# A hybrid decoder step on one core: operands laid out by the host, wide logits, V sums by head pair, pages among the q tiles

## The chip, the cores and the metric

One core of a Trainium2 chip. The time is the device time of one launch in microseconds, median of three runs: 1452.26 (1451.49 to 1453.10). Rearranging inputs and outputs in numpy on the host is outside it.

## What is computed

One layer on 256 prompt tokens and 32 new tokens (8 sequences of 4), T = 288 together, all in float32: RMSNorm, an input projection to q, k, v (8 heads of 128) and u (1024), block-sparse attention, a pooling mixer on u, an output projection, RMSNorm, a SwiGLU feed-forward of width 5632, a last RMSNorm. Each new token attends to a cache of 2048 keys in 16 pages of 128, from which it takes the best 3 of 8 blocks of 256 keys by the mean key, and to its own block.

```python
k_past = cache_k[page_table].reshape(DB, past, H, D)
k_mean = jnp.mean(kb.astype(jnp.float32), axis=2)
idx, valid = moba_select(qh, q_pos, k_mean)            # top 3 blocks by q . k_mean
s_sel = einsum('bhqd,bhqjkd->bhqjk', q, k_sel) * scale - slope * dist
p = softmax(concatenate([s_sel, s_own]))
o = einsum(p_sel, v_sel) + einsum(p_own, v_own)
...
x = x + concatenate([a, p]) @ w_out
x = x + (silu(h2 @ w_gate) * (h2 @ w_up)) @ w_down
```

The kernel reads every page: all K and V pages of the 8 sequences are 256 pages of 512 KB, 134 MB; the weights are 189 MB.

## The kernel before

Weights come as 360 tiles of 512 KB (`tile_at`), in one order that all engines follow: 16 for q (T_Q), 48 for k, v and u (T_KVU), 16 + 16 for the output projection (T_OP, T_OA), 264 for the feed-forward (T_FF). Each lands in `w_raw` (RAW = 4 slots, 6 in the feed-forward); ScalarE rounds it to `w_hi` (line 610), VectorE takes the rest to `w_lo` (line 877), and TensorE runs 24 matmuls of 288 columns, three to a product (`w_tile`, lines 1504 to 1506). A slot is free for its next load when `w_used` has counted the tile (`slot_free`).

All loads are issued by SyncE, one after the other, each behind its own wait: a wait for a slot holds up everything behind it. The order is that of the `block.sync` part: tables and vectors, x, the q tiles with eight K pages among tiles 6 to 13 (line 493), kvu tiles, then `load_v(0)`, `load_v(1)`, and from line 504 one pass for each unit n: `load_k(n + 2)` when the logits of unit n are done, a V unit when the V sums two units back are done, kvu tiles two units ahead. A unit is four pages of one sequence; K and V are buffered two units deep.

x comes token-major and is turned by TensorE (`x_turned`, 48 transposes) and copied by VectorE (`x_taken`); so are the vectors and the pooling history. q of the new tokens is replicated to four row groups (`replicate_q`, `qrep`, `pad_q`).

For unit (i, j) VectorE turns the four K pages in 32x32 blocks (`turn_k`, line 918). `logits` then runs 4 x 4 x 4 matmuls of 32 rows, 32 columns of q and 256 keys into four banks, one for each row group, which `scaled_logits` adds up. `values(i - 1, j - 1)` runs 8 matmuls (K = 128, 32 columns of probabilities, 512 of V) into banks 6 and 7, four column groups, one to a page; `combine` picks each head's rows with 8 matmuls. A float32 matmul stands as two in the rows. At j = 0 the previous sequence is finished: `block_sums`, `select_blocks` (a chain of twelve small VectorE operations), `joint_max`, exponential, `p_turned`. Between these stand the kvu tiles (units 0 to 23), whose results `take_block` moves out of banks 0 and 1, then the eight heads of the prompt (units 24 to 31), with the mixer's matmuls. The end of the last sequence lies among the T_OP tiles. New K, V and u rows are turned to token-major (`rows_turned` on TensorE for V and u, `turn_keys` on VectorE for K) and stored.

## Time and profile before

| | |
|---|---|
| median of three runs | 1452.26 us |
| profiled execution: span, first to last instruction | 1449.9 us |
| what lies around the span, against the median | 2.4 us |
| TensorE, weight loads, VectorE, ScalarE, GpSimd busy | 1394.4, 1294.3, 901.0, 501.0, 111.7 us |
| moved by the transfers | 334.4 MB, mean 231 GB/s |

Matmuls overlap, so busy time of TensorE is that in which at least one was under way, not a measure of its load. Times in the rows are us from the start of the span. PE is TensorE, PEld its weight loads, DVE VectorE, ACT ScalarE, SPq SyncE's queue; a line number is that of the code.

### The profile page before, as it was taken

What the parts mean: (1) busy time and instruction counts of PE and PEld (TensorE: products, weight loads), DVE (VectorE), ACT (ScalarE), POOL (GpSimd) and SP (SyncE); (2) the same over time, 40 slices, a digit from 0 to 9 for tenths busy, and PEclk for the clock granted to TensorE, in tenths of its full rate; (3) what the DMA queues carried; (4) which work ended last, traced back from release to release, by engine and by line L of the source; (5) the groups of instructions that cost most, each with busy time, mean ns of one, the idle gap of its engine ahead of it and who ended that gap; (6) DMA issues with size and microseconds to landing.
All of it is one profiled execution on the core that took longest, in us unless ns stands there. A gap on an engine that the chain in (4) does not pass through costs nothing.

```text
span 1449.9 us, 34103 instructions
## 1 busy us (share of the span) xinstructions
PE 1394.4 (96%) x13900; PEld 1294.3 (89%) x13900; DVE 901.0 (62%) x1355; ACT 501.0 (35%) x663; POOL 111.7 (8%) x180
## 2 busy tenths in 40 slices
PE   6998998998998999999999999999999999999998
PEld 5986777776756799999999999999999999999997
DVE  4678767767777555787555554546464645555556
ACT  4412122112134234544343433333333333333334
POOL 3226510000000000300000000000000000000002
PEclk9999999999999999999999999999999999999999
DMA  6788999999999855655555555555555555555552
GB/s 215 246 308 305 386 400 400 401 401 392 387 395 375 292 178 179 198 166 190 172 164 165 168 162 171 160 171 161 168 164 166 167 162 170 160 170 162 167 167 95
DMA packets 165096, 334.41 MB, mean 231 GB/s; under 512 B 10335, under 2 KB 54680, under 8 KB 164991
## 3 DMA queue, kind: packets, MB, share of 16 engines
q1 hardware_dynamic: 164999, 333.06, 68.1%
q8 instruction: 68, 1.11, 0.3%
q14 instruction: 29, 0.24, 0.0%
HBM read 328.10 MB, written 5.27 MB: 230 GB/s over the span
## 4 chain that ended last, share of the span: by engine, by line
PE 79%; SPq 10%; DVE 4%; issue 3%; DMA 3%; ACT 1%; DVEq 0%; ACTq 0%
PE banks L1504 24%; PE banks L1505 24%; PE banks L1506 24%; SPq L444 3%; SPq L448 3%; PE banks L1622 2%; SPq L466 2%; PE banks L1604 2%; DVE kpage L918 2%; DMA kpage<-in_cache_k 1%; PE banks L1512 1%; SPq L436 1%; DMA w_raw<-in_w_in 1%; PE banks L1688 0%; SPq L521 0%
## 5 line engine op out<-in xcount | busy, mean ns | idle before, releaser
L877 DVE TENSOR_TENSOR w_lo<-w_raw,w_hi 128x1024 fp32r<-128x1024 f32 x360 | 440.8, 1230 | 423.0 <-ACT w_hi L610 421.7
L1504 PE MATMUL banks<-hh,w_hi 128*128 128x288 f32 x2176 | 647.6, 298 | 3.0 <-DVE w_lo L877 1.8
L1505 PE MATMUL banks<-hl,w_hi 128*128 128x288 f32 x2176 | 645.6, 297 | 0.0
L1506 PE MATMUL banks<-hh,w_lo 128*128 128x288 f32 x2176 | 643.3, 296 | 0.4 <-issue 0.4
L610 ACT ACTIVATE w_hi<-w_raw 128x1024 fp32r<-128x1024 f32 x360 | 379.0, 1059 | 676.1 <-PE banks L1506 448.3
L1504 PEld LDWEIGHTS banks<-hh,w_hi 128*128 128x128 f32 x2176 | 411.7, 189 | 23.0 <-issue 15.2
L1505 PEld LDWEIGHTS banks<-hl,w_hi 128*128 128x128 f32 x2176 | 411.9, 189 | 0.1
L1506 PEld LDWEIGHTS banks<-hh,w_lo 128*128 128x128 f32 x2176 | 410.8, 189 | 0.0
L1506 PE MATMUL banks<-ah,w_lo 128*128 128x288 f32 x704 | 207.8, 295 | 0.0
L1505 PE MATMUL banks<-al,w_hi 128*128 128x288 f32 x704 | 207.4, 295 | 0.0
L1504 PE MATMUL banks<-ah,w_hi 128*128 128x288 f32 x704 | 206.6, 293 | 0.5 <-DVE al L1323 0.5
L918 DVE STREAM_TRANSPOSE kpage<-kpage 128x1024 f32<-128x1024 f32 x128 | 150.8, 1219 | 21.3 <-DMA kpage<-in_cache_k 20.9
L1504 PEld LDWEIGHTS banks<-ah,w_hi 128*128 128x128 f32 x704 | 132.5, 188 | 0.7 <-issue 0.7
L1505 PEld LDWEIGHTS banks<-al,w_hi 128*128 128x128 f32 x704 | 132.4, 188 | 0.0
L1506 PEld LDWEIGHTS banks<-ah,w_lo 128*128 128x128 f32 x704 | 132.2, 188 | 0.0
L1622 PE MATMUL banks<-kpage,qr 32*32 32x256 f32 x4096 | 94.3, 408 | 17.1 <-DVE kpage L918 14.1
L1622 PEld LDWEIGHTS banks<-kpage,qr 32*32 32x32 f32 x4096 | 61.3, 106 | 44.1 <-DVE kpage L918 20.0
L1436 POOL COPY ssq<-sq 128x288 f32<-128x288 f32 x3 | 3.1, 1023 | 925.9 <-ACT sq L627 925.9
L1604 PE MATMUL banks<-vpage,pT 128*32 128x512 f32 x512 | 62.9, 610 | 6.5 <-DMA vpage<-in_cache_v 5.8
L1265 DVE TENSOR_TENSOR xT<-xT,banks 128x288 f32<-128x288 f32 x176 | 67.8, 448 | 0.0
L1439 POOL TENSOR_TENSOR ssq<-ssq,sq 128x288 f32<-128x288 f32 x41 | 44.9, 1095 | 50.3 <-ACT sq L627 46.4
L1604 PEld LDWEIGHTS banks<-vpage,pT 128*32 128x32 f32 x512 | 17.4, 142 | 33.7 <-issue 26.1
(197 smaller groups left out, 637.6 us busy)
## 6 DMA issues: line engine op xcount, KB each, us to landing
kpage<-in_cache_k SPq DMA_DIRECT2D x128, 512.0 KB, 8.0
vpage<-in_cache_v SPq DMA_DIRECT2D x128, 512.0 KB, 7.2
w_raw<-in_w_gate SPq DMA_DIRECT2D x88, 512.0 KB, 3.6
w_raw<-in_w_up SPq DMA_DIRECT2D x88, 512.0 KB, 3.6
w_raw<-in_w_down SPq DMA_DIRECT2D x88, 512.0 KB, 3.7
w_raw<-in_w_in SPq DMA_DIRECT2D x64, 512.0 KB, 9.6
w_raw<-in_w_out SPq DMA_DIRECT2D x32, 512.0 KB, 4.0
xs<-in_x_prompt SPq DMA_DIRECT2D x4, 512.0 KB, 6.1
```

Of the source, the lines that this page charges most:

```text
L444: idx = sp.value_load(pages[0:1, bass.ds(e, 1)], min_val=0, max_val=pool.shape[0] - 1)
L448: sp.dma_start(kpage[:, n % 2, g, :], page(ck, n // NQUADS, 4 * (n % NQUADS) + g)).then_inc(k_in[n % 2][g], 16)
L610: return nc.scalar.activation(out, in_, ACT.Copy)
L877: V.tensor_tensor(w_lo[:, s, :], w_raw[:, s, :], w_hi[:, u, :].bitcast(F32), ALU.subtract).then_inc(lo_ready, 1)
L918: V.transpose(kpage[:, n % 2, g, :], kpage[:, n % 2, g, :]).then_inc(k_turned, 1)
L1265: ins = V.tensor_tensor(xT[:, m0 + m, :], xT[:, m0 + m, :], bank[4 * quad + m][:, 0:T], ALU.add)
L1439: G.tensor_tensor(ssq[:, :], ssq[:, :], sq[:, c % 2, :], ALU.add).then_inc(sq_added, 1)
L1504: PE.matmul(o, wh, xh[:, c, :], start=start and i == 0, stop=False)
L1505: PE.matmul(o, wh, xl[:, c, :], start=False, stop=False)
L1506: last = PE.matmul(o, wl, xh[:, c, :], start=False, stop=stop and i == len(chunks) - 1)
L1604: last = PE.matmul(OB[x][32 * g:32 * g + 32, :], pT[:, g, bass.ds(j, 32, 4)], vpage[:, n % 2, g, 512 * x:512 * x + 512], start=j == 0, sto ...
L1622: last = PE.matmul(S[32 * x:32 * x + 32, a, :], qr[32 * a:32 * a + 32, at_:at_ + 32], keys, start=j == 0 and c == 0, stop=j == NQUADS - 1 ...
```

## The change

The host now lays everything out as it is used. The 360 weight tiles are one array, each tile 4 KB per partition (`weight_tiles`); before, a tile was read in rows of 2 KB, of 1 KB (kvu) or of 512 bytes (T_OP). x comes feature-major in five parts straight into `xT`; the vectors straight into `gains`; the pooling history straight into `ext`; each K page with the head dimension on the partitions, so `turn_k`, `x_turned`, `replicate_q` and the turns of the vectors and the history are gone. `logits` is 8 matmuls a unit (K = 128, 32 columns of q in a strip padded with zeros, 512 keys), four column groups, into bank 2 or 3 by sequence. `values` is 16 matmuls a unit (K = 128, 256 columns: one pair of heads x and x + 4), into one bank; `combine` is 2. The kvu tiles use two pairs of banks in turn. All 16 first pages (K and V units 0 and 1) are issued among the q tiles 4 to 15, behind a wait for the page table. k, v and u are stored as they lie, two large stores between T_OA tiles, and turned by the host.

```diff
-STRIP = 32
+STRIP = 36
 PAD = 3
 
 OA_ORDER = (2, 3, 0, 1)
 NORM2_ORDER = tuple(range(8, 16)) + tuple(range(8))
-X_AHEAD = 3
-
-K_BLOCKS = [(a, b) for b in range(T // 32) for a in range(4)]
...
+PAGES_AT = {k: (1, 1, 2)[k % 3] for k in range(4, 16)}
...
-        qr = sb("qr", [P, 17 * STRIP], stack=kv_a)
-        qrep = sb("qrep", [P, 32, TS], stack=kv_a)
+        qz = sb("qz", [P, 2, H * STRIP], stack=kv_a)
         pages = sb("pages", [1, NB * NPAGES], I32, stack=kv_a)
-        pick = sb("pick", [P, 2], stack=kv_a)
 
...
-        WB = bank[0:2]
-        S = banks[:, 2:6, 0:2 * P]
+        WB = bank[0:2], bank[4:6]
+        SB = bank[2:4]
         HB = bank[0:2]
-        OB = bank[6:8]
-        XB = bank[4], bank[5], bank[7]
+        OB = bank[6][:, 0:2 * DH]
+        block_bank, max_bank, sum_bank = bank[6][:, 256:264], bank[6][:, 264:268], bank[6][:, 268:269]
+        ml_bank = bank[6][0:32, 272:288]
+        PB, comb_bank = bank[7], bank[7][0:32, 0:DH]
 
...
+            sp.dma_start(gains[:, :], A["gains"]).then_inc(gains_in, 16)
+
+            def load_x(n):
+                a, b = X_PARTS[n]
+                sp.dma_start(xT[:, a:b, :], A["x"][:, a:b, :]).then_inc(x_in[n], 16)
+
+            def load(t, free=True):
+
+                n, _, s, _ = t
                 if free:
                     sp.wait_ge(w_used, slot_free(t))
-                k, w = src.shape[0] // P, src.shape[1]
-                sp.dma_start(w_raw[:, s, 0:k * w].rearrange("p (k n) -> p k n", k=k),
-                             src.rearrange("(k p) n -> p k n", p=P)).then_inc(w_in_s[s], 16)
-
+                src = w_d[n] if isinstance(n, int) else w_d[bass.ds(n, 1), :, :].rearrange("a p c -> (a p) c")
+                sp.dma_start(w_raw[:, s, :], src).then_inc(w_in_s[s], 16)
+
+            for k in range(RAW):
+                load_x(k)
+                load(tile_at(T_Q + k), free=False)
+            load_x(RAW)
+            sp.dma_start(tab[:, :], A["tables"]).then_inc(tab_in, 16)
             sp.dma_start(pages[:, :], A["page_table"].rearrange("b n -> (b n)").rearrange("(a n) -> a n", a=1)
                          ).then_inc(pages_in, 16)
+            sp.dma_start(ext[:, :, :, :], A["hist"]).then_inc(hist_in, 16)
+            sp.wait_ge(pages_in, 16)
...
+            first_pages = iter([(load_k_page, 0, g) for g in range(4)] + [(load_k_page, 1, g) for g in range(4)]
+                               + [(load_v_page, 0, g) for g in range(4)] + [(load_v_page, 1, g) for g in range(4)])
+            for k in range(RAW, 16):
+                load(tile_at(T_Q + k))
+                for _ in range(PAGES_AT[k]):
+                    load_page, n, g = next(first_pages)
+                    load_page(n, g)
...
-                    sp.wait_ge(tok_act, 2)
-                    sp.wait_ge(tok_dve, 2)
-                    for part in range(2):
-                        sp.dma_start(vp[part * P:(part + 1) * P, :, :], vtok[:, :, P * part:P * part + P]
-                                     ).then_inc(vtok_stored, 16)
+                    sp.dma_start(wpool[:, :, :, :], A["w_pool"]).then_inc(wpool_in, 16)
...
+                    sp.dma_start(O["pool_sample"], ext[:, :, :, :]).then_inc(pool_stored, 16)
+                    sp.dma_start(O["pool_prompt"], u_last).then_inc(pool_stored, 16)
...
+            sp.wait_ge(z_ready, 24)
+            sp.dma_start(O["k_new"], z[:, ZK:ZK + H, :]).then_inc(kv_stored, 16)
+            sp.dma_start(O["v_new"], z[:, ZV:ZV + H, :]).then_inc(kv_stored, 16)
...
-            def osb_low(b):
-                act.wait_ge(v_done, NQUADS * b + NQUADS)
-                if b:
-
-                    act.wait_ge(comb_done, b)
-                copy(osb[:, 0:512], OB[0][:, :]).then_inc(o6_taken, 1)
...
-            def x_taken(c):
-                dve.wait_ge(xT_in, c + 1)
-                V.tensor_copy(xT[:, c, :], XB[c % 3][:, 0:T]).then_inc(x_ready, 1)
...
-            def turn_k(i, j, pages_=range(4)):
-                n = NQUADS * i + j
-                for g in pages_:
-                    dve.wait_ge(k_in[n % 2][g], 16 * (n // 2) + 16)
-                    V.transpose(kpage[:, n % 2, g, :], kpage[:, n % 2, g, :]).then_inc(k_turned, 1)
...
-            dve.wait_ge(rep_in, 1)
-            for x in range(2):
-                V.tensor_copy(qrep[:, 16 * x:16 * x + 16, :],
-                              OB[x].rearrange("p (s t) -> p s t", t=TS)).then_inc(rep_taken, 1)
-            dve.wait_ge(rep_taken, 2)
...
+            own.link(V.memset(qz[:, :, :], 0.0))
 
             def pad_q(b):
-                V.tensor_copy(qr[:, PAD:PAD + 16 * STRIP].rearrange("p (s q w) -> p s q w", q=NQ, w=4)[:, :, :, 0],
-                              qrep[:, :, NQ * b:NQ * b + NQ]).then_inc(qr_ready, 1)
+                for e in range(2):
+                    V.tensor_copy(qz[:, b % 2, :].rearrange("p (e x s) -> p e x s", e=2, x=4)
+                                  [:, e, :, PAD + 16 * e:PAD + 16 * e + 16].rearrange("p x (q w) -> p x q w", w=4)[:, :, :, 0],
...
                 dve.wait_ge(qk_done, NQUADS * b + NQUADS)
                 if b:
                     dve.wait_ge(pt_in, b)
-                own.did(V.tensor_reduce(d4[:, :, :].rearrange("p a u -> p (a u)"),
-                                        S.rearrange("p a (s k) -> p s a k", s=4), AX.XY, ALU.add))
-                for e in range(2):
-                    for a in range(4):
-                        keys = slice(32 * a, 32 * a + 32)
-                        own.did(V.scalar_tensor_tensor(ss[:, :, keys],
-                                                       S[:, a, P * e:P * e + P].rearrange("p (n i) -> p n i", n=4),
-                                                       pick[:, e:e + 1], (past_bias, ss)[e][:, :, keys],
-                                                       ALU.mult, ALU.add))
-                    own.settle()
-                    if e == 0:
-                        own.link(V.tensor_scalar(d2[:, :], d4[:, 0, :], pair[:, 0:1], None, ALU.mult))
-                own.link(V.scalar_tensor_tensor(d2[:, :], d4[:, 1, :], pair[:, 1:2], d2[:, :], ALU.mult, ALU.add))
+                own.did(V.tensor_reduce(d2[:, :], SB[b % 2].rearrange("p (u k) -> p u k", u=2), AX.X, ALU.add))
+                own.did(V.scalar_tensor_tensor(ss[:, :, :], SB[b % 2].rearrange("p (n r) -> p n r", n=4), SCALE,
+                                               past_bias, ALU.mult, ALU.add))
+                own.settle()
                 V.tensor_tensor(dn[:, :, :], d2[:, :].unsqueeze(1).to_broadcast([P, 4, 2]),
...
+                V.tensor_copy(osb[:, :, :], OB.rearrange("p (e d) -> p e d", e=2)).then_inc(o_taken, 1)
...
-            def x_turned(c):
-                if c >= 3:
-                    pe.wait_ge(x_ready, c - 2)
-                if c == KC // 2:
-                    pe.wait_ge(x_half_in[1], 48)
-                for n in range(3):
-                    rows = P if n < 2 else TS
-                    last = turn(XB[c % 3][:, P * n:P * n + rows], xs[0:rows, n, P * c:P * c + P], rows)
-                last.then_inc(xT_in, 1)
...
-            def replicate_q():
-                pe.wait_ge(rep_table, 1)
-                for c in range(2):
-                    pe.wait_ge(quad_taken[c], QT0)
-                for c in range(4):
-                    last = PE.matmul(OB[c // 2][:, 256 * (c % 2):256 * (c % 2) + 256],
-                                     rep_w[:, c, :, :].rearrange("p a i -> p (a i)"),
-                                     z[:, ZQ:ZQ + H, TP:T].rearrange("p (e x) t -> p x e t", e=2),
-                                     start=True, stop=True)
-                last.then_inc(rep_in, 1)
-
...
-                for x in range(2):
-                    for g in range(4):
-                        last = PE.matmul(OB[x][32 * g:32 * g + 32, :], pT[:, g, bass.ds(j, 32, 4)],
-                                         vpage[:, n % 2, g, 512 * x:512 * x + 512], start=j == 0,
-                                         stop=j == NQUADS - 1)
+                if j == 0 and b:
+                    pe.wait_ge(o_taken, b)
+                for g in range(4):
+                    for x in range(4):
+                        heads = vpage[:, n % 2, g, :].rearrange("p (e x d) -> p e x d", e=2, x=4)
+                        last = PE.matmul(OB[32 * x:32 * x + 32, :], pT[:, g, bass.ds(j, 32, 4)], heads[:, :, x, :],
+                                         start=j == 0 and g == 0, stop=j == NQUADS - 1 and g == 3)
                 last.then_inc(v_done, 1)
...
             def logits(b, j):
                 n = NQUADS * b + j
-                pe.wait_ge(k_turned, 4 * n + 4)
+                pe.wait_ge(k_in[n % 2], 64 * (n // 2) + 64)
                 if j == 0:
-                    pe.wait_ge(qr_ready, b + 1)
-                    if b:
-                        pe.wait_ge(dn_ready, b)
-                for c in range(4):
-                    for a in range(4):
-                        for x in range(4):
-                            at_ = STRIP * (4 * c + x) + PAD - j
-                            keys = kpage[32 * a:32 * a + 32, n % 2, :, :].rearrange(
-                                "p n (e x c i) -> p e x c n i", e=2, x=4, c=4)[:, :, x, c, :, :]
-                            last = PE.matmul(S[32 * x:32 * x + 32, a, :], qr[32 * a:32 * a + 32, at_:at_ + 32], keys,
-                                             start=j == 0 and c == 0, stop=j == NQUADS - 1 and c == 3)
+                    pe.wait_ge(qz_ready, 2 * b + 2)
+                    if b >= 2:
+                        pe.wait_ge(dn_ready, b - 1)
+                keys = kpage[:, n % 2, :, :].rearrange("p n (h r) -> p n h r", h=H)
+                for e in range(2):
+                    for x in range(4):
+                        h = x + 4 * e
+                        at_ = STRIP * h + PAD - j
+                        last = PE.matmul(SB[b % 2][32 * x:32 * x + 32, :], qz[:, b % 2, at_:at_ + 32], keys[:, :, h, :],
+                                         start=j == 0 and e == 0, stop=j == NQUADS - 1 and e == 1)
                 last.then_inc(qk_done, 1)
 
             def kvu_tile(n):
                 m, r = n // 4, n % 4
-                if r == 0 and m:
-
-                    pe.wait_ge(z_ready, 2 * m)
-                w_tile(tile_at(T_KVU + n), CW, range(4 * r, 4 * r + 4), WB, hh, hl, r == 0, r == 3)
+                if r == 0 and m >= 2:
+
+                    pe.wait_ge(z_ready, 2 * m - 2)
+                w_tile(tile_at(T_KVU + n), CW, range(4 * r, 4 * r + 4), WB[m % 2], hh, hl, r == 0, r == 3)
...
-                for h in range(H):
-                    last = PE.matmul(OB[0][0:32, 0:DH], headsel[:, h, :], osb[:, DH * h:DH * h + DH],
-                                     start=h == 0, stop=h == H - 1)
+                pe.wait_ge(o_taken, b + 1)
+                for e in range(2):
...
+    def tile(w, r0, rows, c0, cols):
+        return w[r0:r0 + rows, c0:c0 + cols].reshape(rows // P, P, cols).transpose(1, 0, 2).reshape(P, TE)
+
+    tiles = [tile(w_in, 256 * (k % 8), 256, 512 * (k // 8), 512) for k in range(16)]
+    tiles += [tile(w_in, 512 * (n % 4), 512, 4 * AW - CW * (n // 4 + 1), CW) for n in range(48)]
+    tiles += [tile(w_out, AW, AW, P * k, P) for k in range(KC)]
+    tiles += [tile(w_out, 256 * (k % 4), 256, 512 * OA_ORDER[k // 4], 512) for k in range(16)]
+    tiles += [tile(w_gate, 256 * ((k + 4) % 8), 256, 0, 512) for k in range(8)]
+    for g in range(NG):
+        tiles += [tile(w_up, 256 * k, 256, 512 * g, 512) for k in range(8)]
+        if g < NG - 1:
+            tiles += [tile(w_gate, 256 * k, 256, 512 * g + 512, 512) for k in range(8)]
+        tiles += [tile(w_down, 512 * g + 256 * (k % 2), 256, 512 * (k // 2), 512) for k in range(8)]
+    return np.stack(tiles)
+
...
+        "x": x.reshape(T, KC, P).transpose(2, 1, 0),
+        "gains": np.concatenate([v.reshape(-1, P) for v in vectors], 0).T,
+        "hist": np.pad(hist, ((0, 0), (0, 0), (0, 0), (0, NQ))),
+        "cache_k": a["cache_k"][0].transpose(0, 3, 2, 1).reshape(-1, P, AW),
+        "cache_v": a["cache_v"][0].reshape(-1, P, AW),
+        "page_table": a["page_table"],
+        "w_pool": a["w_pool"][0].reshape(4, 2, P, 256).transpose(2, 0, 1, 3),
+        "weights": weight_tiles(a["w_in"][0], a["w_out"][0], a["w_gate"][0], a["w_up"][0], a["w_down"][0]),
+    }
...
```

## Rows read from the trace of the kernel before

**Rows 1.** The page: the span, TensorE's busy line, and GB/s in 40 equal slices.

```profile
span 1449.9 us, 34103 instructions
...
PE 1394.4 (96%) x13900; PEld 1294.3 (89%) x13900; DVE 901.0 (62%) x1355; ACT 501.0 (35%) x663; POOL 111.7 (8%) x180
...
GB/s 215 246 308 305 386 400 400 401 401 392 387 395 375 292 178 179 198 166 190 172 164 165 168 162 171 160 171 161 168 164 166 167 162 170 160 170 162 167 167 95
```

**Rows 2.** Stretches: busy us (instructions) of each engine, granted clock, share of transfer engines, GB/s.

```profile
126.00:160.00 34.00, 32.44 (x525) 26.78 (x501) 25.89 (x36) 6.26 (x8) 24.16 (x55) 0.95 0.83 288
...
160.00:380.00 220.00, 204.65 (x3362) 161.32 (x3365) 157.25 (x240) 42.59 (x53) 14.65 (x30) 0.98 1.04 400
...
247.00:251.00 4.00, 2.08 (x16) 1.85 (x14) 3.89 (x4) 0.00 (x0) 0.00 (x0) 1.00 1.06 372
...
251.00:261.00 10.00, 9.84 (x184) 7.62 (x185) 7.80 (x9) 2.12 (x2) 0.00 (x0) 1.00 1.04 408
...
700.00:1400.00 700.00, 700.00 (x5304) 700.00 (x5303) 379.22 (x513) 260.94 (x293) 0.00 (x0) 1.00 0.54 166
```

**Rows 3.** Transfers from 240 to 280 us: GB/s in 40 slices of 1 us.

```profile
GB/s 430 410 430 393 418 418 404 373 364 369 382 399 410 406 418 397 418 410 413 404 405 377 365 392 391 400 410 414 389 418 422 415 411 393 399 381 389 384 411 393
```

**Rows 4.** SyncE's queue in time: start, length of issue (with its waits inside), line, transfer, count.

```profile
79.19 7.99 SPq L466 DMA_DIRECT2D vpage<-in_cache_v  x8
...
100.53 3.60 SPq L448 DMA_DIRECT2D kpage<-in_cache_k  x4
...
153.09 4.21 SPq L448 DMA_DIRECT2D kpage<-in_cache_k  x4
...
215.81 8.16 SPq L448 DMA_DIRECT2D kpage<-in_cache_k  x4
...
460.68 18.57 SPq L466 DMA_DIRECT2D vpage<-in_cache_v  x12
```

**Rows 5.** The page's issues: count, KB each, median us from issue to landing.

```profile
w_raw<-in_w_gate SPq DMA_DIRECT2D x88, 512.0 KB, 3.6
...
w_raw<-in_w_in SPq DMA_DIRECT2D x64, 512.0 KB, 9.6
```

**Rows 6.** TensorE in time, opening to unit 4: start, us, line, operation, what ended idle.

```profile
15.60 0.58 PE L1504 MATMUL banks<-hh,w_hi 128*128 128x288 f32 x1 [1.82 <-DVE w_lo L877]
...
87.83 2.53 PE L1622 MATMUL banks<-kpage,qr 32*32 32x256 f32 x116 [1.79 <-DVE qr L967]
...
124.84 2.76 PE L1622 MATMUL banks<-kpage,qr 32*32 32x256 f32 x128 [1.98 <-DVE kpage L918]
...
132.75 0.38 PE L1583 MATMUL banks<-dm,tab 128*128 128x4 f32 x2 [1.56 <-DVE dm L1009]
```

**Rows 7.** TensorE in time, the end of attention: last V sums of sequence 6, combine, turns.

```profile
476.27 1.95 PE L1604 MATMUL banks<-vpage,pT 128*32 128x512 f32 x16
...
481.65 1.93 PE L1638 MATMUL banks<-osb,tab 128*32 128x128 f32 x16
...
499.64 1.03 PE L1512 MATMUL banks<-tab,ssq 128*32 128x128 f32 x8
```

**Rows 8.** The page's costliest groups: busy us, mean ns of one, idle before.

```profile
L918 DVE STREAM_TRANSPOSE kpage<-kpage 128x1024 f32<-128x1024 f32 x128 | 150.8, 1219 | 21.3 <-DMA kpage<-in_cache_k 20.9
...
L1604 PE MATMUL banks<-vpage,pT 128*32 128x512 f32 x512 | 62.9, 610 | 6.5 <-DMA vpage<-in_cache_v 5.8
...
L1604 PEld LDWEIGHTS banks<-vpage,pT 128*32 128x32 f32 x512 | 17.4, 142 | 33.7 <-issue 26.1
```

**Rows 9.** ScalarE and VectorE in time, the first weight tile.

```profile
10.99 1.28 ACT L613 ACT_TABLE_LOAD   x1 [10.99 <-DVE xT L908]
...
12.29 0.96 ACT L613 ACTIVATE hh<-xT,gains 128x288 fp32r<-128x288 f32 x2
...
13.15 1.04 ACT L610 ACTIVATE w_hi<-w_raw 128x1024 fp32r<-128x1024 f32 x1
...
14.23 1.23 DVE L877 TENSOR_TENSOR w_lo<-w_raw,w_hi 128x1024 fp32r<-128x1024 f32 x1 [0.43 <-ACT w_hi L610]
```

357 lines of the change are left out of this document (106 added, 251 removed).

## The prediction

> **What bounds the kernel now.** I read the page first [rows 1]. TensorE is called 96% busy, but the GB/s line falls into two parts: some 400 GB/s from slice 5 to slice 13, about 165 afterwards. So I cut the span in two. Late part [rows 2]: between 700 and 1400 us TensorE is never idle, 5304 matmuls in 700 us are 0.132 us each, a weight tile of 24 matmuls takes 3.17 us, and the transfers run at 166 GB/s. That part is bound by TensorE, the change touches nothing of it, and I leave it as it is. Early part [rows 2]: from 160 to 380 us the transfers run at 400 GB/s, share 1.04 (packets overlap, so it is full), while TensorE is idle 15 us of 220. SyncE's queue [rows 4] shows the same: the issue of 4 pages takes 3.60 us when nothing holds it, 8.16 when the rings are full, and a w_in tile lands a median 9.6 us after its issue, a w_gate tile of the same size 3.6 [rows 5]. So **the middle is bound by the transfers**: faster matmuls and a VectorE without transposes give nothing there except where they let transfers start earlier. The opening, units 0 to 6, and the end of attention are not at full rate.
>
> I call four K pages (2.10 MB) with their eight heads a unit: 32 units, 4 to a sequence; "kvu" tiles are the 48 tiles of w_in after q.
>
> **Prices.** (a) Logits: now 128 matmuls of 32x32x256 in 2.76 us [rows 6]. The new ones are 16 matmuls (8, each counted twice as the rows do) of K=128, M=32, N=512, side by side in four column groups: exactly the form of today's V sums, 16 in 1.95 us [rows 7]. I take 1.9. Bounds: 1.8, since no row has that form faster, and, if nothing overlaps, four times it. (b) V sums: 32 matmuls of N=256 instead of 16 of N=512, the same columns. 1.9, at most 2.3. (c) combine: 16 matmuls in 1.93 us [rows 7] become 4: minus 1.4 us each, and the turns of u for its stores (499.64 [rows 7], a like one at 509.6) go: 1.8 us in all. (d) VectorE loses 128 transposes of 1.22 us [rows 8], nearly always beside transfers; cover gone, nothing is late for it. What counts is their lag: a landed K page waited 1.2 to 4.6 us before logits could free its buffer. (e) Layout: the window with the kvu rows of 1 KB ran at 372 GB/s, the one with pages alone, 4 KB, at 408 [rows 2]. All tiles are now 4 KB per partition, so I take 408 for everything; bounds 400 (the present mean) and 420 (slices reach 430 [rows 3]). 
>
> **The sum**, in us from the span's start.
>
> Opening. Now x is turned on TensorE: ScalarE's table load starts at 10.99 [rows 9], the first weight matmul at 15.60, and the first logits run at 87.83 [rows 6]. After: gains, two chunks of x (0.29 MB) and tile 0 are issued by about 2, with 0.82 MB to land. x lands near 4.5; then table load 1.28, two hh copies 0.96, w_hi 1.04, w_lo 1.23 [rows 9]: first matmul 9.2. Sixteen tiles at 3.17 are 50.7. I add 1.2 for the sum of squares ahead of tile 8, and 1.7 because tile 4 is issued only when the page table is in, near 17.5 (5.2 MB lie ahead of it), lands near 21 and needs 2.4 more. Two kvu tiles: 6.3. First logits: **69.2**, 18.6 earlier. The replicated q (8 matmuls, then copies, 84.1 to 87.8) is gone; q's new padding hides under the kvu tiles. SyncE's queue there: three weight tiles and four pages are 3.67 MB, 9.0 us at 408, against 9.5 us of TensorE, so it just fits. The eight V pages that held up the kvu tiles (issued from 79.19 [rows 4], in front of those tiles) are in by then.
>
> Units 0 to 3: four logits (7.6) and six tiles (19.0) are 26.7, plus 1.7 for tile 6 behind K pages: unit 4 at 97.6, now 124.84 [rows 6]. Unit 4: 1.9 + 0.3 + two tiles 6.4 + the turn of the probabilities 0.8, plus 2.3 for VectorE's selection chain between the two tiles (today 132.75 waits 1.56 for it [rows 6]): unit 5 at 109.3. Its logits end at 111.2 and release K unit 7; from **113.4** on transfers have work without a gap.
>
> Middle. From there to the landing of V unit 27: 25 K units and 26 V units (107.0 MB), 34 kvu tiles (17.8), w_pool (1.05), the stored history (0.6), four w_out tiles (2.1): 128.6 MB, at 0.408 MB/us 315: **428.6**. Is TensorE's lane shorter? A unit with two kvu tiles needs 1.9 + 1.9 + 6.3 = 10.1 us, and one in four some 4 more for selection and turn, 11 on average; its transfers, 5.24 MB, 12.9. It is. Units 24 to 30 (heads) need 10.2 to 11 on TensorE by today's pieces less 0.8 for logits, against 10.3 of transfers: about even, so I add 1. The V sums of unit 27 end at **431.5**; today they end at 478.2 [rows 7].
>
> End. From there the last 16 + 16 tiles of w_out and the feed-forward are TensorE's: 1449.9 − 478.2 = 971.7 today. Minus two combines 2.8, minus 1.8 for the rows, plus 1.5 for V unit 30, which is loaded right behind a faster lane, and for the stores of k and v (2.4 MB between two w_out tiles): 968.6. Span 1400; the profiled time above the span was 2.4 (median 1452.3 against 1449.9), so **1402**: 50 us or 3.4% faster. The first 27 of these are won by unit 4, the rest in units 4 to 27.
>
> **Rivals.** A, the forecast (1393 to 1410). For it: the byte sum holds for the kernel now: from the issue of K unit 8 at 153 to the use of V unit 27 at 476 [rows 4, 7] the same kind of sum gives 124 MB in 323 us, 384 GB/s, the shortfall being stretches of short rows and of waiting.
> B, **the opening is held up by its own pages**: weight tiles share the rings with 16 pages. Alone a tile may take 6.6 us to land before TensorE waits (three tiles 9.5 minus 2.9 of issue and splitting); behind pages today's median is 9.6 [rows 5]. Then each tile costs (9.6 − 6.6)/4 = 0.8, twelve tiles 10: 1412. Against it: in today's opening pages and tiles together leave the tiles in time.
> C, **the wide matmuls don't overlap their weight loads** (slower). Place: every unit. Price: loads of 0.142 us [rows 8] in line, 16 for logits and 32 for V sums: 2.3 and 4.5, lane 10.1 to 16.9 against 12.9 of transfers, +4 for 22 units and more for the first: some 1490. It decides from a lane of 15.2, since only 50/22 = 2.3 us above 12.9 eats the gain, that is 100 ns a load. Against it: today's V sums show 16 loads and matmuls in 1.95 us, 0.12 apart, although each matmul lasts 0.61 [rows 7, 8]; the halved N of the V sums is the untested part. The Trainium skill, page "TensorE: Matmul & The Clock Gate", section The mechanism, says that a weight load overlaps running matmuls only in other row groups; the new form has all four row groups in each matmul, so by it this rival is the forecast. The rows of the V sums, of that very form, speak against the rule.
> D, **the transfers are not full after all**: between 126 and 160 they ran at 288 GB/s [rows 2], because TensorE and the selection chain, not the rings, set the pace. If that comes again (10 us) and the rate stays at 400 (6), less what overlaps: 1415. Idle gaps of TensorE belong here: now 15 us of 220 idle, then some 20%; the granted clock was 0.95 of 2.4 GHz on average in the first of these stretches and 0.98 in the second, so a part of each ran at the 1.2 GHz level after TensorE had waited, and 1.00 from 700 us [rows 2]. In the even units 24 to 30 a lower clock costs directly, some us; in the others it has 2.7 us of cover a unit.
> E, faster still: 420 GB/s and no added waits, 1388.
>
> **Numbers.** A 0.56, B 0.16, D 0.18, E 0.05, C 0.04, something that makes the change idle 0.01. Most likely 1402. The range goes from E to past D with some of both rates: 1387 to 1421. About 0.2% is what a measurement of this kernel can tell: faster 0.95, same 0.01, slower 0.04.
>
> **What would show it.** First weight matmul near 9, first logits near 69; no stretch under 380 GB/s from about 115 to 425; rate near 408 also in stretches with kvu tiles; 16 matmuls of logits in about 1.9 us and 32 of V sums in at most 2.3; the start of the last V sums of sequence 6 near 429; and the same distance from there to the end, less 3 us. Wrong, if weight tiles wait for DMA in the opening (B), if K buffers are freed late in units 4 to 8 or in the head units (D), or if logits take over 4 us (C).

## The result and the profile after

The changed kernel takes **1419.9 us** (median of 4 runs, 1419.4 to 1422.8), beside 1451.9 us for the kernel before: a ratio of 0.978 (95% interval 0.977 to 0.980), 32 us or 2.2% faster. I had forecast 1402, with 1387 to 1421 as the range. The direction and the range held; the size was 18 us too good. The range held by 1 us: the measured time lies outside the 1393 to 1410 that I had given to the forecast itself, in the part of the range that rival D had opened. The profiled execution has a span of 1421.0 us (its own time 1422.8), against 1449.9 [rows 1].

The page of the kernel after, with the lines that answer to [rows 1, 8]:

```profile
span 1421.0 us, 27163 instructions
...
PE 1347.4 (95%) x10651; PEld 1254.1 (88%) x10651; DVE 713.9 (50%) x1102; ACT 495.8 (35%) x653; POOL 108.9 (8%) x172
...
GB/s 349 291 314 345 413 412 412 413 413 410 344 410 330 232 207 186 194 164 164 165 170 166 162 163 166 170 166 162 164 168 169 164 162 164 168 170 162 163 162 97
...
L1415 PE MATMUL banks<-vpage,pT 128*32 128x256 f32 x1024 | 63.1, 388 | 14.1 <-DMA vpage<-in_cache_v 13.4
L1431 PE MATMUL banks<-kpage,qz 128*32 128x512 f32 x512 | 67.7, 651 | 8.8 <-DMA kpage<-in_cache_k 8.8
```

VectorE lost 187 us of work and TensorE 3249 recorded instructions, yet the span lost only 29. The GB/s line says why: it is flat at 412 or so where [rows 1] had 400. What the reader should look for is where it is not flat: the first four slices, and the one of 344. TensorE now waits 22 us for pages (14.1 and 8.8 us of idle time stand before the V sums and the logits, nearly all of it for them).

The new pieces themselves, TensorE in time (start, us, line, operation, what ended its idle time):

```profile
8.84 0.58 PE L1354 MATMUL banks<-hh,w_hi 128*128 128x288 f32 x1 [8.84 <-DVE w_lo L799]
...
73.51 1.92 PE L1431 MATMUL banks<-kpage,qz 128*32 128x512 f32 x16
...
360.62 1.92 PE L1431 MATMUL banks<-kpage,qz 128*32 128x512 f32 x16
...
448.52 1.97 PE L1415 MATMUL banks<-vpage,pT 128*32 128x256 f32 x32 [1.79 <-DMA vpage<-in_cache_v]
...
492.52 0.62 PE L1446 MATMUL banks<-osb,tab 128*32 128x128 f32 x4
```

The first weight matmul runs at 8.84 instead of 15.60, the first logits at 73.51 instead of 87.83 [rows 6], the last V sums of sequence 6 at 448.52 instead of 476.27, and the combine is 0.62 us instead of 1.93 [rows 7].

**Where the 29 us of span came from.** I read the starts of the logits of units 4, 24 and 31 in both traces, and the end of the last V sums of sequence 6.

| stretch | before | after | won | forecast |
|---|---|---|---|---|
| to unit 4 | 124.8 | 104.0 | 20.9 | 27.2 |
| units 4 to 24 | 262.6 | 256.6 | 5.9 | about 12 |
| units 24 to 31 | 82.3 | 81.0 | 1.4 | about 8 |
| unit 31 to the end of those V sums | 8.5 | 8.9 | -0.4 | 0 |
| from there to the end | 971.7 | 970.5 | 1.2 | 3.1 |

The two forecasts of "about" are my split of the 19.5 us that the prediction gave to units 4 to 27 and to unit 31; it named only their sum, and 10.2 to 11 us of TensorE for each of the seven head units 24 to 30, 71 to 77 us together, of which I take the middle. So three places fell short: the opening by 6, the middle by 6, the head units by 6 to 7; the end is short by another 2. The windows of the kernel after, in the columns of [rows 2]:

```profile
0.00:113.40 113.40, 95.46 (x693) 86.13 (x694) 62.76 (x82) 44.37 (x63) 43.90 (x73) 1.00 0.87 324
113.40:140.00 26.60, 26.60 (x237) 21.12 (x239) 7.58 (x9) 6.90 (x9) 18.17 (x38) 0.94 0.86 321
140.00:360.00 220.00, 190.46 (x1726) 147.80 (x1719) 71.17 (x143) 41.47 (x50) 13.03 (x26) 0.97 1.02 410
360.00:447.50 87.50, 73.11 (x652) 43.85 (x651) 33.19 (x103) 32.06 (x84) 6.41 (x8) 0.88 0.94 367
```

These four lines settle the byte sum. I had said: 128.6 MB from 113.4 us on at 408 GB/s, ending at 428.6. The windows give 130.8 MB (0.321 x 26.6 + 0.410 x 220 + 0.367 x 87.5) and the end near 447.5. The 19 us between are: 5.9 because 26.6 us ran at 321 rather than 413; 9.7 because the head units ran at 367; 1.6 for 410 in place of 413; 5.4 for 2.2 MB that I had not counted before that point; and 3.8 us back, since full rate is 413, not 408. The middle was right as a mechanism. At both of its ends the transfers were not full.

### The profile page after: what moved, and what is told of

Its sections match the earlier page's. It is cut to its first block, busy times and chain, and to the rows that moved or that the text cites. A ratio compares the mean times of both kernels' runs of the same rounds, so it can differ in the third digit from the quotient of the medians.

```text
span 1421.0 us, 27163 instructions
## 1 busy us (share of the span) xinstructions
PE 1347.4 (95%) x10651; PEld 1254.1 (88%) x10651; DVE 713.9 (50%) x1102; ACT 495.8 (35%) x653; POOL 108.9 (8%) x172
## 4 chain that ended last, share of the span: by engine, by line
PE 78%; DMA 11%; SPq 5%; DVE 3%; issue 2%; ACT 1%; ACTq 0%; DVEq 0%
PE banks L1355 24%; PE banks L1354 24%; PE banks L1356 23%; DMA vpage<-in_cache_v 5%; DMA kpage<-in_cache_k 3%; SPq L426 3%; DMA w_raw<-in_weights 3%; PE banks L1415 2%; PE banks L1431 2%; SPq L440 1%; SPq L430 1%; PE banks L1362 1%; DVE w_lo L799 1%; PE banks L1493 0%; ACT w_hi L551 0%
## 5 line engine op out<-in xcount | busy, mean ns | idle before, releaser
L1415 PE MATMUL banks<-vpage,pT 128*32 128x256 f32 x1024 | 63.1, 388 | 14.1 <-DMA vpage<-in_cache_v 13.4
L1431 PE MATMUL banks<-kpage,qz 128*32 128x512 f32 x512 | 67.7, 651 | 8.8 <-DMA kpage<-in_cache_k 8.8
L1415 PEld LDWEIGHTS banks<-vpage,pT 128*32 128x32 f32 x1024 | 39.2, 139 | 38.4 <-DMA vpage<-in_cache_v 16.2
L1431 PEld LDWEIGHTS banks<-kpage,qz 128*32 128x32 f32 x512 | 14.7, 116 | 38.0 <-issue 27.6
L905 DVE TENSOR_TENSOR z<-banks,rstd 128x288 f32<-128x288 f32 x24 | 9.8, 451 | 46.2 <-PE banks L1356 46.2
```

The lines of the kernel that those rows point to most:

```text
L1415: last = PE.matmul(OB[32 * x:32 * x + 32, :], pT[:, g, bass.ds(j, 32, 4)], heads[:, :, x, :], start=j == 0 and g == 0, stop=j == NQUADS - ...
L1431: last = PE.matmul(SB[b % 2][32 * x:32 * x + 32, :], qz[:, b % 2, at_:at_ + 32], keys[:, :, h, :], start=j == 0 and e == 0, stop=j == NQUA ...
```

## The experiments

Each is an edit of the changed kernel unless it says otherwise. The intervals of the ratios are about 0.13% wide on either side, 1.9 us (0.23% for the short rows): two kernels whose intervals meet are not told apart by time, and there the traces must speak. Each trace is of one execution, and the same stretch differs from one to the next: in the seven kernels whose head units are untouched and load all of V (the kernel after, and the page table first, the zeros, the short rows, V pages late, the even tiles, the late start), units 24 to 31 took 79.2 to 81.0 us.

### Are the middle units bound by transfers or by TensorE?

**More TensorE work, same bytes.**

```diff
+    for r in range(2):
         for e in range(2):
             for x in range(4):
...
-                start=j == 0 and e == 0, stop=j == NQUADS - 1 and e == 1)
+                start=j == 0 and e == 0 and r == 0, stop=j == NQUADS - 1 and e == 1 and r == 1)
```

> From the changed kernel: every matmul of the logits of a unit is issued twice into the same sum, so the logits are twice what they should be (the output is not the reference's) and each unit has 1.9 us more of TensorE, 61 us over 32 units. Theory 1 (transfers set units 10 to 21, TensorE and the chain through ScalarE and VectorE set units 0 to 9 and 22 to 31): units 10 to 21 take no longer than now (waits for pages and weights shrink instead), the others pay some 1.9 us each, in all 25 to 38 us, 1445 to 1458 us. Theory 2 (TensorE sets all units, the waits for pages being chance gaps): some 55 to 61 us, 1475 to 1481. Theory 3 (transfers set nearly all units): 10 us or less.

Measured: 1428.6 us (1427.5 to 1430.0), ratio 0.983 (0.982 to 0.985). **61 us more of TensorE cost 8.7 us.** All theories but the third miss: I had given transfers too little. Between the logits of units 4 and 24 lie 254.9 us, 2 less than without the extra work. The stretch from 140 to 340 us, first of the changed kernel, then of this one:

```profile
140.00:340.00 200.00, 175.36 (x1590) 136.51 (x1583) 66.11 (x132) 39.21 (x47) 13.03 (x26) 0.97 1.03 412
```

```profile
140.00:340.00 200.00, 197.06 (x1852) 143.40 (x1851) 67.99 (x133) 39.84 (x48) 15.79 (x30) 1.00 1.03 412
```

TensorE is busy 197 instead of 175 of 200 us, at a granted clock of 1.00 instead of 0.97, and the transfers run at the same 412 GB/s. Part of the extra work went into waits (those for pages fell from 22 to 4.5 us); another part cost nothing because TensorE, with fewer pauses, was no longer granted the 1.2 GHz level now and then. The cost fell where transfers are not full: units 24 to 31 took 87.7 instead of 81.0 us, units 0 to 4 34.7 instead of 30.5, units 4 to 8 50.0 instead of 46.8.

**Fewer bytes, same TensorE work.**

```diff
 sp.wait_ge(v_done, n - 1)
-for g in range(4):
+for g in range(2):
     load_v_page(n, g)
...
-pe.wait_ge(v_in[n % 2], 64 * (n // 2) + 64)
+pe.wait_ge(v_in[n % 2], 32 * (n // 2) + 64)
```

> From the changed kernel: from unit 2 on only two of the four V page quads of a unit are loaded; the V sums take the stale pages for the rest (the output is not the reference's). That is 2 x 0.52 MB less a unit, some 31 MB of 129 MB, 76 us of transfer at 413 GB/s. Theory 1 (transfers set the time of units 10 to 27): the waits for pages and weights (13.4 us for V, 8.8 for K and most of 23.2 for weights) go, and the last V sums of the unit before last end 20 to 35 us earlier, where TensorE's own work takes over as the bound. Theory 2 (TensorE and its chain set the time already, the transfers run just beneath it): at most 8 us. In both cases what follows the V sums stays at some 970 us.

Measured: 1383.0 us (1382.3 to 1384.6), ratio 0.952 (0.951 to 0.954): 37 us less, theory 1 and a little more. Units 4 to 24 took 223.9 us instead of 256.6, and TensorE's waits for pages fell from 22 us to 1.1. Units 4 to 8 took 45.3 us, within the 43.9 to 47.5 of the kernels that load all of V, issue the logits once and start on time: half of the V bytes gives nothing that shows there. But **units 24 to 31 took 80.4 us, against 81.0 with all bytes**: the head units gained nothing from half of V. Something else sets them.

### What sets the head units?

The rows of the kernel after show it around unit 26. TensorE:

```profile
385.31 1.92 PE L1431 MATMUL banks<-kpage,qz 128*32 128x512 f32 x16
388.44 0.49 PE L1466 MATMUL banks<-z 128*128 128x128 f32 x2 [1.21 <-DVE hl L939]
```

and ScalarE and VectorE:

```profile
385.95 0.44 ACT L551 ACTIVATE hh<-nrm 128x288 fp32r<-128x288 f32 x1
386.30 0.39 ACT L629 ACTIVATE px<-px,pm 128x128 f32<-128x128 f32 x1
```

```profile
387.51 0.55 DVE L934 TENSOR_SCALAR px<-px,pl 128x128 f32<-128x128 f32 x2
387.97 0.42 DVE L939 TENSOR_TENSOR hl<-banks,hh 128x256 fp32r<-128x256 f32 x1
```

The exponential of the head stands in ScalarE's order behind the two mixing operations, which wait for TensorE. From its end a chain runs through VectorE to `hl`, and only then may TensorE do the next head's logits (line 1466). Before the change 2.76 us of page logits covered most of this chain; 1.92 us do not. The wait for `hl` was 0.7 us at most before and is 1.2 now, so of the 0.84 us that a unit saves on logits 0.5 to 0.8 come back in each of the three units with this wait.

That is not all of it. The rows of TensorE's waits between the logits of units 24 and 31 (us in total, times, longest), of the kernel before, with the window of these units behind them, and then of the kernel after, whose window stands above (360.00:447.50):

```profile
PE banks L1583 <- DVE dm L1009: 2.7, 2, 2.3
PE banks L1661 <- DVE hl L1059: 1.5, 3, 0.7
PE banks L1578 <- DVE osb L1030: 0.5, 1, 0.5
...
387.40:470.00 82.60, 72.72 (x1324) 48.45 (x1338) 63.87 (x132) 31.38 (x82) 6.42 (x8) 0.94 1.02 380
```

```profile
PE banks L1391 <- DVE dm L891: 4.0, 2, 2.5
PE banks L1466 <- DVE hl L939: 3.6, 3, 1.2
PE banks L1362 <- DVE px L934: 1.7, 1, 1.7
PE banks L1386 <- DVE osb L912: 1.6, 1, 1.6
```

Together with the rows not shown here, TensorE's waits in these units went from 10.5 to 13.5 us. Apart from `hl` they grew in units 24 and 28, where a sequence is finished and the shorter `combine` takes more cover away: unit 24 alone takes 13.9 us where it took 13.2, although its logits and its `combine` are 2.1 us shorter. The mean granted clock of the stretch fell from 0.94 to 0.88. As an estimate from these two rows, 5.5 us more of full clock were missing (0.12 of 87.5 us against 0.06 of 82.6); only a part of that falls on running matmuls. The saving of the wide matmuls in the head units went into these two, waits and clock; how it divides between them is not measured.

**The exponential first.**

```diff
 head_hi(h - 1)
-for r in MIX_AT.get(h, ()):
-    mixed(r)
 if h < H:
     head_exp(h)
+for r in MIX_AT.get(h, ()):
+    mixed(r)
...
-dve.wait_ge(y_in, MIX_AT[6][-1] + 1)
+dve.wait_ge(y_sc, MIX_AT[6][-1] + 1)
```

> From the changed kernel: in the head units, ScalarE takes the exponential of head h before the mixing operations of that unit, not behind them. Theory 1 (the chain logits, exponential, VectorE, head matmul is now longer than the TensorE work that covers it): the waits of TensorE for the head tile (1.2 us each in units 26, 27 and 30, 3.6 us in all) go, units 24 to 31 take some 77 to 78 us instead of 81, and the whole is 3 to 4 us shorter than 1419.9. Theory 2 (the transfers set the head units too): the waits for the head tile go, waits for V pages of the same size come in their place, and the time stays within 1 us.

Measured: 1418.5 us (1416.3 to 1420.7), ratio 0.976 (0.975 to 0.977). The waits for `hl` and `osb` are gone, as both theories say. Units 24 to 31 took 79.8 us, 1.2 less than in the kernel after, but within the 79.2 to 81.0 of the untouched ones. In their place, TensorE in time:

```profile
403.31 3.12 PE L1415 MATMUL banks<-vpage,pT 128*32 128x256 f32 x32 [2.62 <-DMA vpage<-in_cache_v]
```

A wait of 2.62 us for V pages, where the kernel after has 0.25, and the V sums behind it take 3.12 instead of 1.96. The time is 1.4 us shorter, less than can be told. Theory 2 holds for most of it: chain and transfers are neck and neck here.

**Both at once**: the exponential first and half of V.

> Both edits of two earlier kernels: only two of four V page quads a unit from unit 2 on (the V sums take stale pages for the rest, the output is not the reference's), and ScalarE's exponential of head h ahead of the mixing operations. With half of V alone units 24 to 31 took 80.3 us, with the exponential alone 79.8. Theory 1 (in the head units the chain from logits to head tile and the transfers are near each other, so that either alone hides what the other gives): together 76 to 77.5 us, and the whole 3 to 4 us less than the 1383.0 with half of V alone. Theory 2 (the exponential's place is worth its 1 us in any case, the rest is TensorE's own work and the chain of selection in units 24 and 28): 79 us or more, 1382.

Measured: 1378.6 us (1377.7 to 1379.5), ratio 0.950 (0.948 to 0.951), 4.4 us less than with half of V alone. Units 24 to 31: **73.4 us**. The same edit gives 7.0 us with half of V and 1.2 with all of it. Theory 1 is right, and the effect is twice what I expected. It also shows that TensorE's lane here is 73.4 us with one chain shortened; the 71 to 77 that I predicted are there, but only behind this edit and with fewer bytes.

### How much does the opening carry?

**TensorE starts late.**

```diff
+pe.wait_ge(warm_ready, 1)
+for _ in range(80):
+    PE.matmul(bank[6][:, 0:T], ms[:, 0:P], ms[:, :], start=True, stop=True)
 for k in range(16):
```

> From the changed kernel: TensorE runs 80 matmuls of zeros into an unused bank ahead of its first weight tile, which starts some 10 us later than at 8.8. The transfers may start as before, buffers are freed later. Theory 1 (a microsecond of the opening is a microsecond of the whole, as the prediction has it: transfers are full only once units 4 to 6 free buffers): the delay of the first tile reaches the end whole. Theory 2 (TensorE is ahead of the transfers by unit 8, and what is lost in the opening is caught up as the waits for pages shrink): the transfers' loss is only what the buffers could not take meanwhile; at least a third of the delay is gone by unit 24.

Measured: 1451.6 us (1448.1 to 1453.5), ratio 0.999 (0.998 to 1.000). The matmuls of zeros took longer than I meant: the first weight tile starts at 41.43, 32.6 us late. The first logits are at 101.8 (28.3 late), unit 8 at 181.4 (30.6), unit 24 at 390.7 (30.1), the end of the span 29.2 late. All these are against the profile of the kernel after; by the medians the whole is 31.7 us longer. Some 4 us of the 32.6 are made up before the first logits, since the first tile now runs at the 0.13 us spacing and only one tile is late, by 0.3; **from there on nothing is caught up**: theory 1. So the 20.9 us that the change wins up to unit 4, some two thirds of its whole gain, come whole to the end.

**A warm first tile.** The same with 14 matmuls of zeros:

> From the changed kernel: TensorE gets 14 matmuls of zeros into an unused bank before its first weight tile, in the 8.8 us in which it waits for x. Theory 1 (the 24 matmuls of the first tile run 0.24 us apart instead of 0.13 only because TensorE came to them from idling, which the x turns of the kernel before had prevented): they run 0.13 apart, everything up to unit 4 is 2.6 us earlier, the whole 2 to 3 us shorter. Theory 2 (these matmuls are slow because their operands come late): no change in the first tile, none in the time.

Measured: 1421.1 us (1419.8 to 1422.0), ratio 0.978 (0.977 to 0.979): no gain, but the first tile changes as theory 1 has it. Of the kernel after, two windows of TensorE; then the start of the first tile with the zeros ahead:

```profile
8.84:14.60 5.76, 5.76 (x24) 5.76 (x25) 5.76 (x6) 5.52 (x12) 4.80 (x6) 1.00 1.03 418
14.60:20.00 5.40, 5.40 (x43) 5.40 (x42) 5.09 (x6) 2.35 (x5) 2.86 (x3) 1.00 0.86 328
```

```profile
4.73 5.43 PE L1373 MATMUL banks<-ms 128*128 128x288 f32 x21
9.78 0.52 PE L1356 MATMUL banks<-hh,w_hi 128*128 128x288 f32 x1
10.13 0.29 PE L1357 MATMUL banks<-hl,w_hi 128*128 128x288 f32 x1
10.27 0.29 PE L1358 MATMUL banks<-hh,w_lo 128*128 128x288 f32 x1
```

Without the zeros 24 matmuls take 5.76 us, 0.24 each; with them they run 0.13 apart from the second on. But theory 1 is wrong where it says that the turns of x had kept the kernel before from this. There, too, the first tile begins at 15.60 [rows 6] with its matmuls 0.24 apart, 1.82 us after the turns, and only what follows it is faster (kernel before):

```profile
21.02 0.43 PE L1505 MATMUL banks<-hl,w_hi 128*128 128x288 f32 x1
21.25 0.33 PE L1506 MATMUL banks<-hh,w_lo 128*128 128x288 f32 x1
21.42 1.10 PE L1512 MATMUL banks<-tab,xs 128*128 128x128 f32 x6
```

Both kernels pay 5.8 us for their first tile. With the zeros the first tile is 2.6 us shorter, but it starts 0.9 late, since the zeros overrun, and what is left goes into waits for weight tiles (2.3 us up to 73 us, 2.2 in the kernel after, 0.8 in the kernel with the exponential first, whose opening is untouched): the first logits stand at 73.0, against 72.5 in that kernel. Loading, not TensorE, looks like the next limit there; zeros together with an earlier page table, which would show it, were not run.

**The page table first.**

```diff
 sp.dma_start(gains[:, :], A["gains"]).then_inc(gains_in, 16)
+sp.dma_start(pages[:, :], A["page_table"].rearrange("b n -> (b n)").rearrange("(a n) -> a n", a=1)
+             ).then_inc(pages_in, 16)
...
-sp.dma_start(pages[:, :], A["page_table"].rearrange("b n -> (b n)").rearrange("(a n) -> a n", a=1)
-             ).then_inc(pages_in, 16)
```

> From the changed kernel: the page table is loaded right behind the gains, ahead of x and the first weight tiles, so SyncE no longer stops for it behind four tiles. Theory 1 (in the opening the order of issues costs what the prediction's step for it said): the waits of TensorE for tiles 4 to 6 (2.2 us) go, the first logits run at 70.5 instead of 72.5, and since no transfer is full before unit 4 all of it reaches the end: minus 2 us. Theory 2 (the rest of the opening takes the slack up, K pages and weight tiles being late together): the first logits move by less than 0.7 us and the time stays within 1 us.

Measured: 1417.6 us (1415.9 to 1421.7), ratio 0.976 (0.975 to 0.977). The waits for weight tiles between the first and the first logits are gone, and the first logits run at 71.45. Against the other kernels with an untouched opening (71.8 to 72.7, the profile of the kernel after being the latest with 73.5) that is 0.3 to 1.2 us, between the two theories. The time is 2.2 us shorter by the medians, but the intervals of the two ratios just meet (0.9772 and 0.9770), and in its trace unit 5 is no earlier than elsewhere (117.8 us, 117.9 in the kernel after): that these 2 us come to the end is not shown.

**V pages late.**

```diff
-for _ in range(PAGES_AT[k]):
-    load_page, n, g = next(first_pages)
-    load_page(n, g)
+if 6 <= k < 14:
+    load_k_page((k - 6) // 4, (k - 6) % 4)
...
 for k in KVU_AT[0]:
     load_kvu(k)
+for n in range(2):
+    for g in range(4):
+        load_v_page(n, g)
```

> From the changed kernel: only the K pages of units 0 and 1 are loaded among the q tiles, and the V pages of units 0 and 1 again behind the first k, v and u tiles, as in the kernel before. Theory 1 (bytes decide: what isn't moved before unit 4 must be moved when the transfers are full): 4.2 MB more at 413 GB/s, up to 10 us longer, less what the idle transfers between 75 and 120 us still take: 1423 to 1429. Theory 2 (the early pages hold weight tiles up in the opening, as rival B has it, and only that counts): the first logits 1 to 2 us earlier than 72.5 and no loss in the end.

Measured: 1421.0 us (1418.8 to 1424.5), ratio 0.979 (0.978 to 0.981). Theory 2 by its numbers: the first logits come at 70.2, 2.3 earlier than 72.5, and the time is the same. But the 2.3 us are not kept either. From 73 to 104 us the transfers ran at 405 GB/s instead of 309, after 283 instead of 318 up to there: both kernels have moved 33 MB by 104 us. The idle transfers of the opening took the late pages up. Loading eight V pages early, the part of the change that I had counted on to free the kvu tiles, buys nothing that can be measured by itself.

### Does the row length matter?

```diff
+if T_KVU <= n < T_OP:
+    m, r = (n - T_KVU) // 4, (n - T_KVU) % 4
+    c0 = 4 * AW - CW * (m + 1)
+    rows_ = A["w_in"][512 * r:512 * r + 512, c0:c0 + CW]
...
+sp.dma_start(w_raw[:, s, 0:k_ * w_].rearrange("p (k n) -> p k n", k=k_),
+             rows_.rearrange("(k p) n -> p k n", p=P)).then_inc(w_in_s[s], 16)
```

> From the changed kernel: the tiles of k, v and u weights and of the projection are read out of the unpermuted weights, in rows of 1 KB or 512 bytes as before the change; all else stays. Theory 1 (the longer rows are what lifted the transfers from 400 to 413 GB/s): the stretch from 160 to 340 us falls back to some 400 GB/s, unit 22 starts 5 to 7 us later, the whole takes 1424 to 1427 us. Theory 2 (the 400 GB/s before came from the small loads and gaps of that kernel, not from the row length): the rate stays at 412, the time within 1 us of 1419.9.

Measured: 1423.6 us (1422.8 to 1429.4), ratio 0.981 (0.979 to 0.984), 3.7 us longer by the medians, though the two intervals still meet. The stretch from 140 to 340 us:

```profile
140.00:340.00 200.00, 176.77 (x1558) 136.60 (x1557) 64.13 (x128) 39.51 (x47) 11.02 (x24) 0.96 1.04 407
```

407 instead of 412 GB/s (the line of 412 stands above; every kernel with 4 KB rows and all of V that starts on time has 411 to 413), 1.2%; over these 200 us that is 2.4 us. Theory 1 holds in its direction, with 5 of the 13 GB/s that it gave. Only the 30 kvu tiles issued in this stretch, 15.7 of its 81 MB, have the short rows. If the whole loss is theirs, they ran at some 388 GB/s against 412: an estimate, the 65.7 MB of the rest at 412 leaving 40.5 us for them. That is 6%, where I had read 9% from a window of 4 us [rows 2].
### Is a wait for the last weight tile a matter of order?

Behind the logits of unit 23 TensorE waits 4.65 us for the last of the 48 kvu tiles (TensorE in time, kernel after):

```profile
342.05 1.92 PE L1431 MATMUL banks<-kpage,qz 128*32 128x512 f32 x16
...
348.62 0.40 PE L1354 MATMUL banks<-hh,w_hi 128*128 128x288 f32 x1 [4.65 <-DVE w_lo L799]
```

It is the longest wait behind the opening, and SyncE issues this tile at the end of its turn. Two tries to remove it.

```diff
-KVU_COUNT = (2, 1, 1) + (2,) * 19 + (3, 1)
+KVU_COUNT = (2, 1, 1) + (2,) * 21
```

> From the changed kernel: the last four k, v and u tiles are spread 2 and 2 over units 22 and 23 instead of 3 and 1. Theory 1 (the wait of 4.65 us for the last of these tiles at 348.6 us is a matter of order and costs what it shows): units 24 to 31 start 3 to 4 us earlier, 1416 to 1417. Theory 2 (the transfers are full until there, the bytes ahead of V unit 27 are the same, and the wait is only where TensorE meets them): the wait goes or moves, the time stays within 1 us.

Measured: 1422.2 us (1421.1 to 1424.4), ratio 0.979 (0.978 to 0.981). The wait is still there, 4.80 us at 346.1. The time is 2.4 us longer by the medians, with intervals that meet; theory 1 has failed, and theory 2 fits.

### Three chains, and the last tile

**Three edits together**: the exponential first, the page table first, and VectorE's 2.27 us for `qza` moved.

```diff
 rows_out(3)
+q_spread()
 take_values(i - 1)
...
 head_max(0)
-q_spread()
 head_probs(0)
```

> From the changed kernel, three edits together, all the work done: ScalarE's exponential ahead of the mixing operations, the page table loaded behind the gains, and VectorE's clearing and filling of qza (2.3 us) moved from between the maximum and the probabilities of head 0 to its idle time after the copies of v. Theory 1 (in unit 24 no transfer is late, TensorE waits 1.7 and 2.7 us for VectorE's chain): these waits shrink by 2 us together, unit 25 starts 2 us sooner after unit 24, the whole takes 1415 to 1416. Theory 2 (the transfers take it back before unit 31): as long as with the exponential alone, 1418 to 1419.

Measured: **1414.5 us** (1413.8 to 1418.5), ratio 0.975 (0.974 to 0.977): 5.3 us less than the kernel after by the medians, and below it on the ratios' intervals too. Theory 1. Units 24 to 31 took 75.3 us. Unit 24, TensorE in time, first with the exponential alone, then with all three:

```profile
359.73 1.92 PE L1431 MATMUL banks<-kpage,qz 128*32 128x512 f32 x16
...
365.11 0.52 PE L1362 MATMUL banks<-tab,px 128*128 128x128 f32 x3 [1.73 <-DVE px L934]
368.31 0.59 PE L1391 MATMUL banks<-dm,tab 128*128 128x4 f32 x2 [2.69 <-DVE dm L891]
368.76 1.20 PE L1480 MATMUL banks<-ptp,vtok 128*128 128x256 f32 x2
369.75 0.63 PE L1481 MATMUL banks<-ptp,vtok 128*128 128x128 f32 x2
370.32 1.87 PE L1502 MATMUL banks<-z,qza 128*32 128x4 f32 x32
```

```profile
356.32 1.92 PE L1431 MATMUL banks<-kpage,qz 128*32 128x512 f32 x16
...
360.50 0.52 PE L1362 MATMUL banks<-tab,px 128*128 128x128 f32 x3 [0.53 <-DVE px L934]
363.72 0.39 PE L1391 MATMUL banks<-dm,tab 128*128 128x4 f32 x2 [2.70 <-DVE dm L891]
363.96 0.68 PE L1480 MATMUL banks<-ptp,vtok 128*128 128x256 f32 x2
364.48 0.39 PE L1481 MATMUL banks<-ptp,vtok 128*128 128x128 f32 x2
364.79 1.53 PE L1502 MATMUL banks<-z,qza 128*32 128x4 f32 x32
```

From one unit's logits to the next are 11.4 us instead of 13.9. Half of the 2.45 us is the wait for `px`, 1.20 shorter. The other half is clock: the same small matmuls behind the 2.7 us wait take 0.59, 1.20, 0.63 and 1.87 us in the first and 0.39, 0.68, 0.39 and 1.53 in the second. The window from 360 to 380 us has a granted clock of 0.74 in the kernel after and with the exponential alone, and 0.83 here. That the shorter pause before is the reason is not shown: the next kernel has no wait for `px` at all there and yet 0.74. The wait for `dm`, of which I had expected part of the gain, did not move: VectorE's chain for it begins behind `px`, and is as long.

**The last tile first**, on top of these three edits.

```diff
 for n in range(NQUADS * NB):
+    if n + 2 == len(KVU_AT) - 1:
+        for k in KVU_AT[n + 2]:
+            load_kvu(k)
     if n + 2 < NQUADS * NB:
         load_k(n + 2)
```

> From the kernel with the three chains shortened (1414.5 us): the last k, v and u tile is issued ahead of the K pages of unit 23 and the V pages of that turn instead of behind them; the bytes are the same. There TensorE waits 4.64 us for this tile at 344.3 us, and just behind it, from 350 to 360 us, the transfers fall from 410 to some 350 GB/s. Theory 1 (the wait is a matter of order: TensorE stood still, so V buffers came free late and the transfers had nothing to do): the wait falls below 1 us, the dip goes, the whole takes 1411 to 1413. Theory 2 (the bytes ahead of unit 24 are the same, TensorE waits as long for the K pages of unit 23 or for V pages instead): within 1 us of 1414.5.

Measured: 1414.5 us (1412.1 to 1416.0), ratio 0.973 (0.972 to 0.975). The wait for the tile is gone, and so is the dip behind it (409 GB/s from 350 to 360 us). TensorE, around it:

```profile
325.93 3.25 PE L1434 MATMUL banks<-kpage,qz 128*32 128x512 f32 x16 [2.05 <-DMA kpage<-in_cache_k]
...
353.84 3.52 PE L1418 MATMUL banks<-vpage,pT 128*32 128x256 f32 x32 [3.28 <-DMA vpage<-in_cache_v]
```

But it waits 3.28 us for V pages instead, and unit 24 starts at 358.1, no earlier than with the tile behind (356.3). In unit 24 the wait for `px` is gone, but the small matmuls are back at the slow level:

```profile
367.14 1.87 PE L1505 MATMUL banks<-z,qza 128*32 128x4 f32 x32
```

Units 24 to 31 took 77.1 us, 1.8 more than without this edit.

Theory 2: a wait for a transfer within a full stretch is only the place where TensorE meets the bytes. Both kernels with the shortened chains are faster than the two of this case, by 0.4% than the changed one and by some 2.5% than the one before.

## Why the prediction was right in sign and off in size

**What bounds the kernel: right.** The late part is hardly touched: 970.5 us from the V sums to the end where I had 968.6, and 971.7 before. Middle bound by transfers: shown twice, by the doubled logits (61 us of TensorE for 8.7 us) and by half of V (37 us off).

**First weight matmul: right**, 8.84 against 9.2.

**First logits: 73.5 against 69.2, the first term mis-sized.** I priced sixteen tiles at 3.17 us from rows at full clock [rows 2]. The first takes 5.8, as it did in the kernel before, whose trace I could have read: 2.6 us. The waits for tiles and for the sum of squares took 3.6 where I had 2.9, and the two matmuls of that sum, which stand between tiles at 39.53 us, another 0.65. The first matmul's 0.4 goes the other way; some 0.8 us are not traced. A warm first tile would not have made the forecast true: with it the first logits came at 73.0, the rest having gone into a later start and into waits. In the other kernels with an untouched opening they came at 71.8 to 72.7, so a part of the 4.3 us belongs to this one execution.

**Units 0 to 4: 30.5 us against 28.4.** K pages and weight tiles are late by turns there. Unit 4 itself took 13.9 against 11.7; in the other kernels with an untouched start it took 11.6 to 13.8, and the wait for the selection chain is 1.7 to 2.4 (I had 2.3), so the excess is waiting and clock and varies from run to run.

**"From 113.4 on transfers have work without a gap": wrong, 5.9 us.** They ran at 321 GB/s until 140, below the 380 that I had named as a sign of being wrong. This is rival D's place, and its cause: TensorE and the selection chain, not the rings, free the buffers. Half of the V bytes left units 4 to 8 as they were, and doubled logits, 7.7 us more of TensorE, made them 3.2 us longer. The kernel after shows 0.94 of full clock there.

**Rate: right, for a wrong reason.** 408 forecast, 412 to 414 measured. Row length gives 407 to 412, no more. The 400 of the kernel before [rows 2] is therefore in part something else; I did not test what, and its many small pauses for page turns are only a guess. The prediction's "3 us longer" without a gain from row length does not come out of its own terms either: 128.6 MB at 400 instead of 408 GB/s take 6 us more, as rival D has it.

**Heads: the step that failed.** I wrote that units 24 to 30 need 10.2 to 11 us "by today's pieces less 0.8 for logits", about even with 10.3 of transfers, and added 1 us. The pieces were right and their sum was not the time. Subtracting 0.84 us of logits, and 1.3 us of `combine` in units 24 and 28, assumed that nothing was hidden beneath them. Beneath them ran ScalarE's exponential and VectorE's chains; with the cover gone much of the time came back as waits, 13.5 us over these units instead of 10.5, and more of the stretch ran at the lower clock level (0.88 on average instead of 0.94). Half of V leaves 80.4 us, half of V with the exponential first 73.4. So the chain was last here, and the transfers idled behind it: the 32.1 MB from 360 us on would have taken 77.7 us at 413 GB/s and took 87.5. With that chain shortened, waits for pages take its place (79.8 us), yet the transfers are still not full from 360 to 447.5 us (369 GB/s); with the chain of unit 24 shortened as well the same bytes went at 386 GB/s and the units took 75.3 us.

**V sums, logits, combine: right** (1.96, 1.92, 0.62 us against at most 2.3, 1.9, about 0.5). Rival C is refuted: loads and matmuls overlap, 16 of them in 1.92 us with all four row groups in use and 592 ns each. The rule of the Trainium skill, page "TensorE: Matmul & The Clock Gate", section The mechanism, that a load overlaps only in other row groups, does not describe these rows; the same section also lets a load into the background weight buffer go ahead, and no run here shows whether that is what happened.

**Rival B** had its mechanism but not its price: without the eight V pages the first logits come 2.3 us earlier, not 10, and the end is the same. **Rival D**, at 1415, was nearest, and its idle gaps came too, though with 30 of 220 us (13%) rather than 20%: I had given it 0.18 and put its loss between 126 and 160 us, where a third of it was; the larger part was in the head units.

## What to carry to other kernels

Taking work off an engine gives back what it covered: before subtracting a shortened step, look at what ran beneath it on the other engines, and ask which of them is then last. Price the first piece of a stretch from its own rows, not from the mean of later ones. In a stretch bound by transfers count the bytes, and price its two ends apart: there the chains decide, and a late start of the whole is not made up. A wait for a transfer inside a full stretch was no target here, and neither was the dip in the rate behind it: the edit that removed both gained nothing. The waits for another engine's chain in the head units were one: with them shortened, and the page table loaded first, the kernel is 5.3 us faster.

## What was not expected of the hardware

Rates over windows of a few microseconds mislead: one of 4 us in the kernel before gave 372 GB/s, where 200 us with kvu tiles in short rows gave 407 after the change. TensorE's first 24 matmuls ran 0.24 us apart in a window whose granted clock stands as 1.00, later ones 0.13 apart: there the column does not show the level, only the spacing does. A wait can cost more than its length: behind the 2.5 to 2.7 us wait for `dm` in unit 24 the same small matmuls took 1.87 us in some kernels and 1.53 in another. Whether a pause is followed by the lower level differed from run to run in ways that these rows do not settle. With 61 us more of TensorE work the clock rose from 0.97 to 1.00 in the middle; the added work had part of its price back.
